# Feed-forward tails: adaptive sums spread over other stretches, gate rows kept as unsummed rows with their bias added by a transfer

## The reference, cut to what matters

```python
cond = silu(c)
for i in range(4):
    mod = einsum('bd,sde->sbe', cond, ada_w[i]) + ada_b[i][:, None, :]
    shift, scale, gate = split(mod, 3, axis=-1)              # s = 0, 1: two sites a layer, 1024 wide each
    h = x * (1 + scale[0]) + shift[0]
    y = mixer_i(h)
    x = layer_norm(ALPHA * x + (1 + gate[0]) * y, ln_g[i, 0], ln_b[i, 0])
    h = x * (1 + scale[1]) + shift[1]
    y = (silu(h @ w_g) * (h @ w_u)) @ w_out                  # feed-forward
    x = layer_norm(ALPHA * x + (1 + gate[1]) * y, ln_g[i, 1], ln_b[i, 1])
```

## Time and profile before

| | |
|---|---|
| time, median of 3 | 2360.52 us (2359.36 to 2362.55) |
| the profiled execution: time, span | 2366.01 us, 2364.2 us |
| TensorE busy | 2257.6 us (95%), 11911 matmuls |
| VectorE, ScalarE, GpSimd busy | 76%, 49%, 6% |
| mean granted TensorE clock | 0.979 of full speed |
| tails of layers 0, 1, 2: the last `down` ends and the stir begins at | 1350.76, 1648.27, 2025.77 us |

### The profile page before, as it was taken

The page is one execution under the profiler, slowest core; times in us unless marked ns, Lnnn a source line. Parts: engine busy times, 40 slices in busy tenths (PEclk is TensorE's granted clock), DMA queues, the critical chain, the costliest instruction groups (busy, mean ns, idle before and its releaser), DMA issues. The chain is left out here.

```text
span 2364.2 us, 30212 instructions
## 1 busy us (share of the span) xinstructions
PE 2257.6 (95%) x11911; PEld 1906.7 (81%) x11911; DVE 1808.2 (76%) x2130; ACT 1156.1 (49%) x1201; POOL 133.4 (6%) x231
## 2 busy tenths in 40 slices
PE   7999989999999999989999999999998999898997
PEld 7888667888888888878788787887987888797886
DVE  6887587598888888856888777887796888777555
ACT  4443244577767677745343363442652443364432
POOL 2000100000000000000011000110001111000000
PEclk9989988899999999999999999999998999999999
DMA  8844553399999999954699436995643998344652
GB/s 302 262 136 146 174 170 99 138 366 369 367 359 366 359 365 360 364 171 143 202 384 368 167 126 179 384 361 179 188 133 117 307 380 293 127 143 156 189 189 72
DMA packets 347440, 570.93 MB, mean 241 GB/s; under 512 B 69152, under 2 KB 182304, under 8 KB 347296
## 3 DMA queue, kind: packets, MB, share of 16 engines
q1 hardware_dynamic: 326496, 493.45, 61.7%
q0 software_dynamic: 20800, 75.52, 8.5%
HBM read 567.83 MB, written 1.05 MB: 241 GB/s over the span
## 5 line engine op out<-in xcount | busy, mean ns | idle before, releaser
L285 DVE TENSOR_TENSOR st_lo<-st_raw,st_hi 128x2048 fp32r<-128x2048 f32 (+1 forms) x195 | 441.1, 2268 | 123.4 <-ACT st_hi L275 123.2
L275 ACT CAST st_hi<-st_raw 128x2048 fp32r<-128x2048 f32 (+1 forms) x195 | 368.8, 1895 | 241.5 <-PE ps L315 153.2
L285 DVE TENSOR_TENSOR es_lo<-es_raw,es_hi 128x2048 fp32r<-128x2048 f32 x192 | 429.5, 2288 | 73.2 <-ACT es_hi L275 72.9
L313 PE MATMUL ps<-st_hi,sb_h_hi 128*128 128x512 f32 (+1 forms) x1232 | 463.3, 376 | 17.4 <-DVE sb_h_lo L1138 7.9
L315 PE MATMUL ps<-st_hi,sb_h_lo 128*128 128x512 f32 (+1 forms) x1232 | 453.5, 368 | 0.0
L314 PE MATMUL ps<-st_lo,sb_h_hi 128*128 128x512 f32 (+1 forms) x1232 | 453.0, 368 | 0.0
L275 ACT CAST es_hi<-es_raw 128x2048 fp32r<-128x2048 f32 x192 | 357.6, 1914 | 46.5 <-PE ps L315 27.4
L313 PEld LDWEIGHTS ps<-st_hi,sb_h_hi 128*128 128x128 f32 x1232 | 234.4, 190 | 59.9 <-issue 13.5
L315 PEld LDWEIGHTS ps<-st_hi,sb_h_lo 128*128 128x128 f32 x1232 | 234.1, 190 | 38.8
L314 PEld LDWEIGHTS ps<-st_lo,sb_h_hi 128*128 128x128 f32 x1232 | 234.7, 191 | 35.5
L313 PE MATMUL ps<-es_hi,moe_hg_hi 128*128 128x512 f32 x512 | 204.5, 399 | 0.8 <-PEq L61 0.8
(11 more groups left out here) (698 smaller groups left out, 3749.6 us busy)
## 6 DMA issues: line engine op xcount, KB each, us to landing
st_raw<-in_ffn_w_in_dram SPq DMA_DIRECT2D x176, 512.0 KB, 6.8
t_aw<-in_ada_w_dram POOLq DMA_DIRECT2D x144, 512.0 KB, 7.0
es_raw<-in_w_expert_gate_dram SPq DMA_DIRECT2D x64, 1024.0 KB, 8.1
es_raw<-in_w_expert_up_dram SPq DMA_DIRECT2D x64, 1024.0 KB, 7.2
es_raw<-in_w_expert_down_dram SPq DMA_DIRECT2D x64, 1024.0 KB, 7.1
st_raw<-in_ffn_w_out_dram SPq DMA_DIRECT2D x44, 1024.0 KB, 8.7
fb_aw<-in_ada_w_dram SPq DMA_DIRECT2D x39, 512.0 KB, 6.3
hs_raw<-in_w_in_dram SPq DMA_DIRECT2D x36, 512.0 KB, 7.3
```

Of the source, the lines that this page charges most:

```text
L275: act.copy(p.at(self.hi[:, m % self.held, :]), p.at(self.raw[:, n % self.slots, :])).then_inc(self.high, 1)
L285: dve.tensor_tensor(p.at(self.lo[:, m % self.held, :]), p.at(self.raw[:, n % self.slots, :]), p.at(self.hi[:, m % self.held, :]).bitcast(F ...
L313: pe.matmul(out, a_hi, b_hi, start=start, stop=False, skip_group_check=True)
```

## The change

Every tail that prepares a next layer (0, 1, 2):

- Site 0's 16 column sums stay in the last `down` calls (one group of four ahead of them, three beside them); site 1's 16 go behind the last `down` (`column_sums(1, 0)`), where `stir` was for this site, which is gone.
- Of the four gate matmuls one (`next_gate(3, 0)`) stays, behind `turn_hidden`; one (`next_gate(6, 1)`) comes behind `turn_norm(1, 1)`. Both belong to the next layer's site 0. Site 1's row isn't summed here: its two matmuls and two ScalarE copies stand in the next layer's tail (1, 2, 3), ahead of `turn_norm(0, 0)`, which waits for the copies (`row_kept`).
- The gates' thirds are added up in `k.gates` itself. Their bias goes onto partition 0 by two accumulating GpSimd transfers of 4 KB each, behind the last of the 48 steps (`bias_landed`), and the two broadcasts of 512 KB are gone. ScalarE adds the 1 as it copies the sum; VectorE's four `gate_row` are gone.
- The columns are merged one site at a time: site 0 where both were; site 1's sums are added behind `normalise` and its other four steps come behind `divide(1)`, ahead of the next piece's `st_lo`. TensorE waits for `sums_read` before it writes bank 0.

```diff
+def add_sums(k, dve, site, sums):
+    c = k.cols[:, site]
+    return dve.tensor_tensor(c[:, 0:2, :], c[:, 0:2, :], sums.rearrange("p (a k) -> p a k", a=2), ALU.add)
+def merge_columns(k, dve, after, site):
+    c = k.cols[:, site]
+    after(dve.tensor_scalar(c[:, 1, :], c[:, 1, :], 1.0, None, ALU.add))
+    after(dve.tensor_tensor(c[:, 2, :], c[:, 2, :], c[:, 1, :], ALU.mult))
+    after(dve.tensor_tensor(c[:, 3, :], c[:, 3, :], c[:, 1, :], ALU.mult))
+    return dve.tensor_tensor(c[:, 3, :], c[:, 3, :], c[:, 0, :], ALU.add)
...
+        row_banks, row_summed, row_kept = (5, 6) if woven else (1, 3), st.sem("row_summed"), st.sem("row_kept")
...
+            slot = [k.gates[:, (2 * layer + 2 + s) % 3, :] for s in range(2)]
+            third_of = lambda s, third: slot[s] if third == 2 else ada[:, s, third * 1024:(third + 1) * 1024]
...
+            pairs = column_loads(k, A, layer + 1, 0)[:-1] + column_loads(k, A, layer + 1, 1)[:-1]
...
+            if not final:
+                pool.wait_ge(ada_added, N_ADA)
+                for s in range(2):
+                    pool.dma_start(slot[s][0:1, :], A["ada_b_2"][layer + 1, s:s + 1, 2048:3072], accum_op=ALU.add
+                                   ).then_inc(k.bias_landed[s], 16)
             root(2)
             root(3)
...
-                    if i == 0 and t == (not site and not early):
+                    if i == 0 and not site and t == (not early):
                         stir(k, pe, 0, 9)
...
+            if layer:
+                pe.wait_ge(k.bias_landed[1], 16 * layer)
+                for c in range(2):
+                    last = pe.matmul(ps[:, row_banks[c], :], k.ones[:], gate[1][:, c * BANK:(c + 1) * BANK], start=True, stop=True)
+                last.then_inc(row_summed, 1)
             pe.wait_ge(gated, 3)
+            if layer:
+                pe.wait_ge(row_kept, 1)
             turn_norm(0, 0)
             turn_norm(0, 1)
...
-            if not final:
-                pe.wait_ge(ada_added, N_ADA)
-                pe.wait_ge(hid_split, N_BLOCKS - 1)
-                sums = column_sums()
-                ada_gate(3, 0, 0)
+            pe.wait_ge(hid_split, N_BLOCKS - 1)
             w, v = S.take(pe), S.take(pe)
-            down(N_BLOCKS - 2, w, 0, 0, sums)
+            down(N_BLOCKS - 2, w, 0, 0)
             turn_hidden(N_BLOCKS - 1)
             if not final:
-                ada_gate(1, 1, 0)
-                pe.wait_ge(hid_split, N_BLOCKS)
-                ada_gate(0, 0, 1)
+                pe.wait_ge(k.bias_landed[0], 16 * (layer + 1))
+                pe.wait_ge(ada_added, N_ADA)
+                next_gate(3, 0)
+                sums = column_sums(0, 2)
+                next(sums)
             down(N_BLOCKS - 1, v, 0, 0, sums).then_inc(part, 1)
             down(N_BLOCKS - 2, w, 0, 1, sums)
-            down(N_BLOCKS - 1, v, 0, 1, sums).then_inc(part, 1)
-            if not final:
-                pe.wait_ge(ada_kept, 1)
-                ada_gate(3, 1, 1)
+            down(N_BLOCKS - 1, v, 0, 1).then_inc(part, 1)
...
             if not final:
-                pe.wait_ge(ada_kept, 4)
+                for _ in column_sums(1, 0):
+                    pass
+                pe.wait_ge(ada_kept, 1)
                 pe.wait_ge(merged, 1)
                 turn_norm(1, 0)
                 turn_norm(1, 1)
+                pe.wait_ge(gated, 7)
+                next_gate(6, 1)
+                pe.wait_ge(sums_read, 1)
...
+            if layer:
+                act.wait_ge(row_summed, 1)
+                for c in range(2):
+                    last = act.activation(gate[1][:, c * BANK:(c + 1) * BANK], ps[:, row_banks[c], :], ACT.Identity,
+                                          bias=k.ones[:, 0:1])
+                last.then_inc(row_kept, 1)
             modulated(0)
...
-                gate_row(0, 3, 0, 0)
-                gate_row(1, 1, 1, 0)
-                gate_row(2, 0, 0, 1)
...
-                gate_row(3, 3, 1, 1)
...
-                merge_columns(k, dve, after, ps[:, 2, 0:32].rearrange("p (s a k) -> p s a k", s=2, a=2)
-                              ).then_inc(merged, 1)
+                after(add_sums(k, dve, 0, ps[:, 2, 0:16]))
+                merge_columns(k, dve, after, 0).then_inc(merged, 1)
...
                 normalise(1, 1)
+                dve.wait_ge(ada_cols, 2)
+                add_sums(k, dve, 1, ps[:, 0, 0:16]).then_inc(sums_read, 1)
                 divide(1)
+                dve.wait_ge(sums_read, 1)
+                merge_columns(k, dve, after, 1)
                 S.lower(dve, f_end + 2)
```

More of the change, by code:

```diff
@@ L859, in layer_tail @@
         else:
-            ada, aw = st.sb("ada", [P, 2, 3072]), st.sb("aw", [P, 4, 1024])
+            ada, aw = st.sb("ada", [P, 2, 2048]), st.sb("aw", [P, 4, 1024])
+            slot = [k.gates[:, (2 * layer + 2 + s) % 3, :] for s in range(2)]
+            third_of = lambda s, third: slot[s] if third == 2 else ada[:, s, third * 1024:(third + 1) * 1024]
             ada_landed, ada_base = k.aw_landed, layer * 12
             ada_added, ada_cols, ada_rows = st.sem("ada_added"), st.sem("ada_cols"), st.sem("ada_rows")
-            ada_kept, cols_landed, merged = st.sem("ada_kept"), st.sem("cols_landed"), st.sem("merged")
-            pairs = column_loads(k, A, layer + 1, 0) + column_loads(k, A, layer + 1, 1)
+            ada_kept, cols_landed, merged, sums_read = (st.sem(n) for n in ("ada_kept", "cols_landed", "merged", "sums_read"))
+            pairs = column_loads(k, A, layer + 1, 0)[:-1] + column_loads(k, A, layer + 1, 1)[:-1]
             ada_w = [A["ada_w_2"][layer + 1, s] for s in range(2)]
@@ L992, in down @@
                     if beside:
-                        next(beside)
+                        next(beside, None)
                     last = product(pe, ps[:, 4 + 2 * t + c, :], hid_hi[:, b % 2, f, at], hid_lo[:, b % 2, f, at],
@@ L997, in down, with column_sums, next_gate @@
                 return last
[L999 to L1012, removed]
+            def column_sums(s, bank):
+                for i in range(16):
+                    op = pe.matmul(ps[:, bank, i:i + 1], ada[:, s, i * P:(i + 1) * P], k.ones[:, 0:1], start=True, stop=True)
+                    if i == 15:
+                        op.then_inc(ada_cols, 1)
+                    if i % 4 == 3:
+                        yield
+            def next_gate(bank, c):
+                pe.matmul(ps[:, bank, :], k.ones[:], slot[0][:, c * BANK:(c + 1) * BANK], start=True, stop=True
+                          ).then_inc(ada_rows, 1)
             for kind, b, a in order[:-2]:
@@ L1072, in modulated, with keep_gate @@
                                    ).then_inc(scaled, 1)
+            def keep_gate(bank, c):
+                act.wait_ge(ada_rows, c + 1)
+                act.activation(slot[0][:, c * BANK:(c + 1) * BANK], ps[:, bank, :], ACT.Identity, bias=k.ones[:, 0:1]
+                               ).then_inc(ada_kept, 1)
+            if layer:
[4 more added lines that the diff above has]
+                last.then_inc(row_kept, 1)
             modulated(0)
@@ L1089, in _ @@
             if not final:
+                keep_gate(3, 0)
                 S.lift(act, f_end + 2)
@@ L1092, in _ @@
                 modulated(1)
+                keep_gate(6, 1)
         @block.vector
@@ L1183, in _ @@
                     dve.wait_ge(ada_landed[m % 4], 16 * (ada_base + m // 4 + 1))
-                    at = ada[:, s, third * 1024:(third + 1) * 1024]
+                    at = third_of(s, third)
                     if kb == 0:
@@ L1207, in finish_row @@
                                              ALU.mult, ALU.add).then_inc(kept, 1)
-            def gate_row(n, bank, s, c):
-                g = k.gates[:, (2 * layer + 2 + s) % 3, c * BANK:(c + 1) * BANK]
-                dve.wait_ge(ada_rows, n + 1)
-                dve.scalar_tensor_tensor(g, ps[:, bank, :], 1.0, g, ALU.add, ALU.add).then_inc(ada_kept, 1)
-            if not final:
-                gate_row(0, 3, 0, 0)
-                gate_row(1, 1, 1, 0)
-                gate_row(2, 0, 0, 1)
             dve.wait_ge(part, 3)
@@ L4357, in second_block @@
         k.aw_landed = [nc.alloc_semaphore(f"aw_landed{q}") for q in range(4)]
+        k.bias_landed = [nc.alloc_semaphore(f"bias_landed{s}") for s in range(2)]
         k.stream = Stream(nc, own, "st", second_plan(A), UNIT, 4, 3)
```

## The result

The changed kernel takes 2367.49 us (median of 22 runs, 2358.70 to 2370.65), the kernel before, on the same chip, 2362.14 (22 runs, 2359.00 to 2367.06). The ratio is 1.0019, 95% interval 1.0012 to 1.0026: some 4.5 us slower, where 5.0 faster was forecast. Measured again (experiment 10) it gave 1.0013, 1.0002 to 1.0025. Both intervals lie above 1, and both ratios under the 0.2% that the prediction took as the least that can be told from no change. The time lies above the predicted range of 2351.5 to 2362. The profiled execution has a span of 2366.8 us against 2364.2. It took 2368.60 us, where the changed kernel's 22 executions went from 2358.70 us at a mean granted clock of 0.977 to 2370.65 us at 0.972.

The account below looks back on a forecast made before the run. TensorE, busy for 95% of the span, was taken as the bound, with VectorE close behind. Terms -14.4 + 2.2 + 4.8 + 2.4 = -5.0 from 2360.5, with 0.1 for semaphores, gave 2355.6 us; range 2351.5 to 2362.

Parts of the forecast that it names:

- tails, last `add` earlier: In three tails, VectorE's last `add` begins 4.8 us earlier each, as TensorE's last `down` ends sooner: -14.4 us.
- second merge: At the tail's end, four VectorE steps between `divide(1)` and the last `st_lo`, without cover: 0.74 us each, +2.2.
- site 0 of layers 1 to 3: Row matmuls and ScalarE copies ahead of the stir and turns add uncovered work, 1.45 to 1.9 us a layer: +4.8.
- clock at the turns: Behind site 1's sums on end the clock halves in about eight tails of ten, slowing turns: 0.8 a tail, +2.4.
- Removed from the last `down` calls: Two gate matmuls and three groups of sums go, `down` starts 0.38 earlier: TensorE ends 4.96 us earlier per tail.
- rows at half clock elsewhere end soon in dense work: Argument against half clock lasting through the next stage's opening, of which two thirds are dense products.
- Rivals 3 and 4: Half clock reaches the middle of the next stage's opening (2363.2 us, chance 0.16) or its end (2370.7 us, chance 0.08).
- Rival 3: Half clock for half of the opening's 6 us, less slack, 2.5 a tail: +2.7 in sum, 2363.2 us, chance 0.16.
- rival 2: Site 0's row sums cost less than half by overlapping the stir, clock held: about -9.7, 2350.8 us, chance 0.08.
- At nothing: Items put at zero cost: accumulating bias transfers landing before TensorE needs them, saved broadcasts, `keep_gate`; semaphores at most 0.1 us a stage.
- Rival 5: VectorE's piece holds `hid_lo` longer, losing the 0.38 and leaving part of 4.1: at worst +1.2; no chance given.
- three signs that the prediction named for being wrong: The stir overlaps the row copies, the clock is 1.00 in all tails, or TensorE waits for `bias_landed`.

Follow-up runs that it names:

- experiment 10: The changed kernel itself, unedited, measured again on the chip of the other runs: ratio 1.0013 to the kernel before.
- experiment 1: Changed kernel plus seven stirs (14 wide passes) in TensorE's wait for `hid_lo`, nothing taken away: 0.9954 of the kernel before, 2353.95 us.
- experiment 7: Kernel before, with only site 1's sums moved behind the last `down` in place of `stir` and columns merged one site at a time: 0.9942, 2350.87 us.
- experiment 12: Changed kernel plus seven stirs in the wait for `hid_lo` and two stirs behind each of site 1's four groups of sums: 1.0007, 2364.14 us.
- experiment 2: Changed kernel with all four groups of site 0's sums on end in the wait for `hid_lo`, none beside `down`'s products: 0.9959, 2353.91 us.
- experiment 11: Changed kernel: gate rows, stirs and sums fill the `hid_lo` wait, sums and stirs mixed behind last `down`, row sums and second merge moved later: 0.9952, 2350.58 us.

## Why the prediction was wrong

The sum, term by term, in us for three tails or three sites. "Measured" is by traces: the tail terms from experiment 1, in which `down` ran at full clock, the clock in `down` from its tails against those of the changed kernel (there the last `add` alone is 11.1 later, and the turns are 0.2 cheaper).

| term | forecast | measured |
|---|---|---|
| tails, last `add` earlier | -14.4 | -14.25 (22.9 - 18.15 = 4.75, three times) |
| second merge | +2.2 | +2.05 (`divide` to next stage 8.55, before 7.87) |
| site 0 of layers 1 to 3 | +4.8 | +5.6 (1.69, 2.08, 1.83) |
| clock at the turns | +2.4 | +1.6 (1.06, 0.49, 0.01) |
| clock in the last `down` | 0 | +10.85 (4.03, 3.22, 3.60) |
| final tail | 0 | -0.25 (24.86 to 24.61) |
| sum | -5.0 | +5.6 |

The clock at the turns is the distance from the last `add` to `divide`: 6.36, 5.79 and 5.31 against 5.3 before. The measured sum stands against 4.5 by the first ratio, with 1.7 on either side. It is one trace's: the second trace of the changed kernel has tails of 110.4 in sum and not 108.4.

**The step that failed** is the one under "Removed from the last `down` calls". It worked out that `down` can't start until VectorE has made `hid_lo`, about 2 us behind the turn, and took 0.38 us of gain for it. That was right: the wait ended 0.46 earlier in both traces of the changed kernel, and 4.75 came out where 4.8 was forecast once the clock held. But the same sentence means that a TensorE which had kept itself busy there with wide gate passes would now stand idle for over a microsecond between two groups of one-column sums. The working named the wait and never asked it the question it asked further on, under "The clock", of the sums behind the last `down`: what the granted clock does behind narrow work. There the rows already showed it falling in narrow sums that weren't even idle. So the clock in the last `down` calls was put at nothing without a reason, and it measured 3.2 to 4.0 us a tail. Its length too stood in the trace of before, against "rows at half clock elsewhere end soon in dense work": that fall lasted 6.8 us, 5.0 of them dense 512-column products behind the sums, as this window shows:

```profile
116.60:123.40 6.80, 6.80 (x22) 5.74 (x23) 4.14 (x9) 1.20 (x3) 0.00 (x0) 0.50 0.63 47
```

**"In the tails of before the sums were mixed with products and the clock held"** was true and was read too widely. What held it there was also that the wait was 0.54 long with 512-column passes on both sides; experiment 7 keeps that, and it holds. Which of the two does it, the shorter wait or the wide passes around it, no run separates.

**The clock's price at the turns** was about right (1.6 for 2.4), and so was that it comes in nearly every tail: it came in all three, with a price from 0.01 to 1.06. That the sizes agree is in part luck, as single tails ranged so widely. Rivals 3 and 4 gave times on the right side, by a wrong mechanism: they put the slow stretch into the opening, and there the window of after from 1360.80 on has a clock of 1.00, and the products stand 0.12 apart. Rival 3's own sum is off besides: half of 6 us less the slack of 1 is 2.0 a tail and not 2.5, which would give 2361.7.

**Site 0** was mis-sized by 0.3 a site: from the first row matmul to the stir it took 3.33 (1445.81 to 1449.14), where 3.05 was taken from another pair; ScalarE's two copies of 512 take 1.26 together, where one of 1.115 was the model. The sign, the place and the lack of an overlap (rival 2) were as forecast. **The merge** was right, 0.7 a tail. **At nothing**: TensorE shows no wait for `bias_landed`. Rival 5 didn't occur, as the 4.75 shows. None of the three signs that the prediction named for being wrong came, since none of them asked for a fall in `down`; what failed was its first sign of being right, a last `down` that ends some 5 us earlier (in layer 0 it ended 0.1 earlier, and 4.9 earlier in experiment 1).

Of the miss of 11.9 us between 2355.6 and 2367.49, 1.6 is the kernel before itself, whose median of 22 runs is 2362.14 and not 2360.52.

## What to carry to other kernels

When work is taken out of TensorE's row, write down what is left around each wait: a wait that wide passes used to cover may afterwards stand among one-column passes, and at half clock the dense products behind it cost most of what was removed (here 10.85 us against 14.25). Seven stirs without use bought the gain back, and moving only the sums behind which there are short turns and a wait did as well with less (experiment 7, 0.9942). Filling is worth it only in a wait that the trace shows; where there was none (experiment 12) the tails got 3.4 to 3.9 us longer. And a term read from one trace belongs to that execution: look where its time stands among the others' (experiment 1's was 7.5 us above its median).

## What the runs showed of the hardware

A TensorE that the profile shows as busy without a gap can lose its full clock: sums of one column on end (experiment 2, busy 2.80 of 2.80 us ahead of the fall), and also such sums with pairs of wide stirs between them (experiment 12, 3.90 of 3.90). Dense 512-column products do not bring it back at once: in the changed kernel they ran at half clock for 6.8 to 13.7 us behind the wait. How long it stayed down differed between tails that are alike in the program, 10.2, 6.8 and 6.8 us in one trace and 10.2, 13.7 and 6.8 in the other, so a term for it is a range and not a number. What a fall cost followed its length: against +18.15 at full clock the last `add` came 3.2 us later behind a fall of 6.8, 4.8 behind one of 10.2 and 6.1 behind one of 13.7. Why the same mixture of three groups held the clock in two tails of experiment 11 and not in the third can't be told from these traces.
